# Eight time-step products on whole fp32 tiles that GpSimd adds, in place of sixteen on high and low parts

## What is computed

```python
h = rmsnorm(x, p['norm1_g']) * (1 + sc1) + sh1
u, q, k, v, z, xbc, dt_raw = split_sizes(h @ p['w_in'], IN_SIZES)
...
dt = jax.nn.softplus(dt_raw.reshape(b, n, 2, SSD_HEADS) + p['ssd_dt_bias'])
```

## Time and profile before

| | |
|---|---|
| median of 3 runs | 1295.12 us (1294.97 to 1297.24) |
| span of the profiled execution | 1295.7 us |
| TensorE busy | 1275.4 us |
| VectorE busy | 1078.2 us |
| ScalarE busy | 652.1 us |
| GpSimd busy | 183.8 us |

### The profile page before, as it was taken

One profiled execution on the slowest core, in us unless ns is written; L12 is line 12 of the kernel. 1 busy time (PEld: TensorE's weight loads), 2 busy tenths in 40 slices (PEclk: granted clock), 3 DMA queues, 4 the chain that ended last, 5 costly groups with the idle time before them and its releaser, 6 DMA issues.

```text
span 1295.7 us, 20368 instructions
## 1 busy us (share of the span) xinstructions
PE 1275.4 (98%) x7736; PEld 1228.9 (95%) x7736; DVE 1078.2 (83%) x1984; ACT 652.1 (50%) x1098; POOL 183.8 (14%) x187
## 2 busy tenths in 40 slices
PE   6999999999999999999999999999999999999997
PEld 5999899999999999999999988999999999999997
DVE  5899978878987999999968998877988799999433
ACT  5643555555566454543375336555555754554332
POOL 0067000002210000001103910000042000000110
PEclk9999999999999999999999999999999999999999
DMA  9566436544443444458735662464435254444431
GB/s 360 186 235 205 161 115 217 172 150 142 150 146 114 147 163 144 166 177 278 237 111 180 223 211 84 168 233 142 141 129 195 83 167 141 163 136 164 152 127 56
DMA packets 60481, 216.26 MB, mean 167 GB/s; under 512 B 7104, under 2 KB 9408, under 8 KB 58848
## 3 DMA queue, kind: packets, MB, share of 16 engines
q1 hardware_dynamic: 56224, 199.38, 45.4%
q0 software_dynamic: 4016, 15.39, 3.9%
q10 hardware_dynamic: 144, 0.20, 0.0%
HBM read 211.17 MB, written 3.77 MB: 166 GB/s over the span
## 4 chain that ended last, share of the span: by engine, by line
PE 83%; DVE 8%; ACT 5%; issue 2%; DMA 2%; SPq 0%; DVEq 0%; ACTq 0%; POOLq 0%
PE acc L1044 25%; PE acc L1046 25%; PE acc L1045 25%; DVE cv L2001 2%; DVE wl L1820 1%; PE mixes L1315 1%; DMA crow_late<-in_cvec_rows_dram 1%; PE mixes L1219 1%; DMA x<-in_xp_dram 1%; ACT th L1445 1%; ACT hh L1434 1%; PE mixes L1249 1%; DVE junk_late L1909 1%; PE misc L1032 1%; ACT cv L1445 0%
## 5 line engine op out<-in xcount | busy, mean ns | idle before, releaser
L1044 PE MATMUL acc<-hh,wh 128*128 128x384 f32 x1519 | 516.0, 340 | 0.6 <-DVE wl L1820 0.2
L1046 PE MATMUL acc<-hh,wl 128*128 128x384 f32 x1519 | 507.9, 334 | 0.0
L1045 PE MATMUL acc<-hl,wh 128*128 128x384 f32 x1519 | 507.7, 334 | 0.0
L1820 DVE TENSOR_TENSOR wl<-raw,wh 128x1024 fp32r<-128x1024 f32 (+1 forms) x276 | 342.0, 1240 | 72.9 <-ACT wh L1409 71.7
L1409 ACT ACTIVATE wh<-raw 128x1024 fp32r<-128x1024 f32 (+1 forms) x276 | 287.0, 1041 | 134.2 <-PE acc L1046 131.5
L1044 PEld LDWEIGHTS acc<-hh,wh 128*128 128x128 f32 x1519 | 285.2, 188 | 8.5 <-issue 3.4
L1045 PEld LDWEIGHTS acc<-hl,wh 128*128 128x128 f32 x1519 | 285.3, 188 | 1.5
L1046 PEld LDWEIGHTS acc<-hh,wl 128*128 128x128 f32 x1519 | 285.2, 188 | 0.0
L2001 DVE SCALAR_TENSOR_TENSOR cv<-acc,prm,cv 128x1 f32<-128x1 f32 (+1 forms) x416 | 153.7, 411 | 9.0 <-ACT cv L1572 1.9
L1046 PE MATMUL acc<-ah,wl 128*128 128x384 f32 x352 | 117.6, 334 | 0.0
L1044 PE MATMUL acc<-ah,wh 128*128 128x384 f32 x352 | 117.6, 334 | 0.0
(11 more groups left out here) (320 smaller groups left out, 1670.4 us busy)
## 6 DMA issues: line engine op xcount, KB each, us to landing
raw<-in_wstream_dram SPq DMA_DIRECT2D x248, 512.0 KB, 3.8
rawm<-in_wstream_dram SPq DMA_DIRECT2D x80, 512.0 KB, 4.3
raw<-in_wstream_dram SPq DMA_DIRECT2D x32, 448.0 KB, 3.7
head<-in_whead_dram SPq DMA_DIRECT2D x8, 1024.0 KB, 15.1
rowf<-runs_dram POOLq DMA_DIRECT2D x12, 256.0 KB, 4.2
rowb<-runs_dram POOLq DMA_DIRECT2D x12, 256.0 KB, 4.8
crow_late<-in_cvec_rows_dram POOLq DMA_DIRECT2D x2, 1024.0 KB, 6.3
crow<-in_cvec_rows_dram POOLq DMA_DIRECT2D x2, 1024.0 KB, 5.3
```

What stands on the lines that cost most here:

```text
L1044: mm(out, sh, mhi, start=start, stop=False)
L1045: mm(out, sh, mlo, start=False, stop=False)
L1046: return mm(out, sl, mhi, start=False, stop=stop)
L1820: tt(wl[:, s, 0:n], raw[:, raw_slot(u), 0:n], wh[:, s, 0:n].bitcast(F32), ALU.subtract).then_inc(lo_done, 1)
```

## The change

GpSimd gets a new step `whole_tiles`, at its places `u` = 4 to 7 in each layer (`WHOLE0`), two tiles at each: it adds `hh` and `hl` of a tile to a plain fp32 tile, in `gates[6]` to `gates[12]` and `ot[0]`, which are free then. `time_steps` waits for all eight and does eight products on them. The names of the semaphore and of the tiles are new; nothing else moves.

```diff
--- before.py
+++ after.py
@@ -246,6 +246,7 @@
 SLOT_PW, SLOT_X, SLOT_A, SLOT_S, SLOT_Y = 4, 14, 17, 17, 19
 SLOT_LN = SLOT_X + 1
 SLOT_WDC = 7
+WHOLE0 = 4
 POOLING = (UU0 + 4, UU0 + 6, UU0 + 9, UU0 + 12)
 
 Y_SLOTS = 2
@@ -466,6 +467,7 @@
         mix7 = mixes[:, 2, :]
 
         dtc = gates[:, 13, :]
+        whole = [gates[:, 6 + k, :] for k in range(KT - 1)] + [ot[:, 0, :]]
 
         head_bank = [(mix7, mix5)[p % 2][:, 8 * (p // 2):8 * (p // 2) + 8] for p in range(KT // 2)]
         wt_bank = (acc[3], misc[:, :])
@@ -568,6 +570,7 @@
         lam_exp = sem("lam_exp")
         lam_sum = sem("lam_sum")
         wd_hi = sem("wd_hi")
+        whole_made = sem("whole_made")
         u_in = sem("u_in")
         pooled = sem("pooled")
         pads = sem("pads")
@@ -763,6 +766,19 @@
                     last = nc.gpsimd.memset(ut[:, :, c0:c1], 0.0)
                 last.then_inc(pads, 1)
 
+            def whole_tiles(l, k0):
+
+                if k0 == 0:
+                    if l:
+                        group_done(pool, l - 1, NG - 1)
+                    else:
+
+                        pool.wait_ge(scale_ready, KT // 2)
+                    pool.wait_ge(h_lo, count(l, NSPLIT, SP_N1 + KT - 1))
+                for k in (k0, k0 + 1):
+                    nc.gpsimd.tensor_tensor(whole[k], hh[:, k, :].bitcast(F32), hl[:, k, :].bitcast(F32), ALU.add) \
+                        .then_inc(whole_made, 1)
+
             def pooling(l, j):
 
                 tmp = [gates[:, 20:22, :].rearrange("p a t -> p (a t)")[:, 0:UW],
@@ -831,6 +847,8 @@
                         lo(l, u + AHEAD)
                     if u == 4:
                         clear_pads(l)
+                    if WHOLE0 <= u < WHOLE0 + 4:
+                        whole_tiles(l, 2 * (u - WHOLE0))
                     if u in POOLING:
                         pooling(l, POOLING.index(u))
                     if u == MIX0 + 8:
@@ -1164,11 +1182,10 @@
                 misc_turn(l, M_DT)
 
                 pe.wait_ge(par_ready, l + 1)
-                for half, src in enumerate((hh, hl)):
-                    for k in range(KT):
-                        g = 32 * (k % 4)
-                        last = mm(mz[g:g + 32, :], wd[:, k, :], src[:, k, :].bitcast(F32),
-                                  start=(half == 0 and k < 4), stop=(half == 1 and k >= 4))
+                pe.wait_ge(whole_made, KT * (l + 1))
+                for k in range(KT):
+                    g = 32 * (k % 4)
+                    last = mm(mz[g:g + 32, :], wd[:, k, :], whole[k], start=(k < 4), stop=(k >= 4))
                 last.then_inc(misc_done, 1)
 
             def time_transposes(l):
```

## The result

| | median of 5 runs | span of the profiled execution |
|---|---|---|
| before | 1295.78 us (1294.97 to 1297.24) | 1295.7 us |
| after | 1304.28 us (1303.87 to 1304.47) | 1302.2 us |

The ratio of the runs is 1.0066, with a 95% interval of 1.0056 to 1.0077: slower by 8.5 us, above the forecast range (1293.2 to 1299.4), and above the 1298.9 of rival 1 as well.

The account below looks back on a forecast made before the run. TensorE, busy 1275.4 of 1295.7 us, was taken as the bound. Layer 0 +2.6, layer 1 +1.5 and saving -2.2 gave +1.9 us: 1297.0 us, no change that can be told, range 1293.2 to 1299.4.

Parts of the forecast that it names:

- rival 1: Layer 0: small parameter instructions take turns with adds too, `nlam` 3.3 us late, layer 0 costs 4.5; 1298.9 us, chance 0.28.
- the start of layer 0: Layer 0, XBC stage: adds 1 and 2 make `nlam` 1.2 us late, and with it the first evacuation, taps and `wl`.
- The start of the adds: GpSimd, layer 0: adds begin once the pads are cleared, by 47.73, after a set-up taken as short.
- the price for a small one: Small VectorE parameter instructions, layer 0: may or may not take turns, between nothing and 0.87 us per add then running.
- the 50.5: Sign in layer 0: the prediction is wrong if `nlam` comes past 50.5.
- the walk: Layer 0 up to unit 6: `nlam` 1.2, `wl` of unit 4 0.5, `xbc` behind it 0.9 late; +2.6 us.
- Layer 1: XBC stage of layer 1: unit 3 waits 1.2 us longer; unit 6 is 1.5 us late, including the 1.2.
- The lock rule: GpSimd adds and VectorE instructions with two SBUF inputs exclude each other for a whole instruction; 0.87 us per add met.
- The saving: Time steps: eight products fewer, 1.31 us a layer, 1.1 kept; 2.2 us in all, bounds 2.0 and 2.6.
- Rivals 3 and 4: Adds do not hurt, 1292.5 to 1292.9 us, chance 0.08; time-step saving is not there, 1299.2 us, chance 0.04.
- The set-up: GpSimd instruction between pads and first add, layer 0: between nothing and 26.9 us, taken as short.
- rival 2: Layer 0: set-up of 8 us or more, adds too late to harm, cost 0.4 us; 1294.8 us, chance 0.12.

Follow-up runs that it names:

- own_wait: The changed kernel, with GpSimd also waiting ahead of the adds for the semaphore of its own memsets; 1297.66 us in a single run.
- lam_sum: The changed kernel, with the adds also waiting for VectorE's sum over `lamt`; 1297.87 us timed, ratio 1.0019 to the kernel before.
- after_params: The changed kernel, with GpSimd's adds also waiting until that layer's parameter instructions are through (`nlam`); 1298.70 us, ratio 1.0024.
- eight_only: The changed kernel without adds or the wait for them, eight products on the high parts `hh` only; 1293.18 us, ratio 0.9981.
- small_mid: `after_params` plus one small two-input VectorE sum between the first taps and `wl`, in the midst of the adds; 1299.96 us in a single run.
- sum_behind: The changed kernel, with VectorE's product and sum over `lamt` put behind the four halvings, GpSimd unchanged; 1305.24 us in a single run.
- late6: The changed kernel, with each layer's adds waiting until VectorE has made the weights `wl` of unit 6; 1293.04 us, ratio 0.9982.
- one_gap: The changed kernel, with GpSimd waiting for its own semaphore once per layer, behind the first add; 1301.05 us in a single run.

## Why the prediction was wrong

**The step that failed** is the one on the start of layer 0: "Adds 1 and 2 then hold off the last small parameter instructions: `nlam` [...] comes 1.2 us late". The start of the adds was right: 45.34 is, to 0.02, the forecast 47.73 less the 2.41 by which this execution is ahead. But the step took for granted that a held VectorE instruction gets its turn behind the add in progress, and the price for a small one was bounded by 0.87 for each add then running. It got its turn behind the eighth, 7.6 us late. `nlam` ended at 53.72, past the 50.5 that the prediction named as a sign of its being wrong, TensorE waited 7.05 us at unit 4, and its clock fell to half. The layer 0 stretch cost 9.26 us where 2.6 was forecast: 7.2 at the wait, and 2.0 net behind it at half clock. Rival 1 looked at the right instructions and thought of turns with them (3.3 us late); turns are not what happened.

**With that step as assumed, the term is right.** Where GpSimd stops ahead of its first add (`own_wait`), two small instructions wait for one add each, and the walk comes out term by term: `nlam` ends 1.5 late (forecast 1.2), the first `wl` loses 0.5 (0.5) and the `xbc` behind it 0.8 (0.87). Layer 0 costs 2.84, for the 2.6 forecast; `lam_sum` costs 2.93, and its 1297.87 stands beside the 1297.0. In `after_params` the price is 3.99, of which 1.5 is clock: that is a term which the prediction put at nothing. From the earlier trace rows it took the clock for full; what a wait of 2 us does to it, no row of before showed. That `own_wait` and `lam_sum` come so near the forecast is luck in one respect: their waits of 1.3 to 1.4 us left the clock full.

**Layer 1** was forecast at +1.5 and cost 1.67, of which 1.2 at unit 3, as forecast: `wl` pieces of 1.35 and 1.21, then a `wl` of 1.58 and an `xbc` of 1.37, and a wait of 1.60 at unit 3 in place of 0.40. The lock rule of the Trainium skill (SBUF — State Buffer, Who interferes with whom) agrees with the trace here, and with `after_params`. In layer 0 it is right that the two exclude each other, but blocking the second to issue, for one instruction, is not enough to give the 7.80 us: the halving was recorded 0.02 ahead of the first add, and 0.11 with three more memsets, and had to let eight of them pass.

**The saving** was forecast at 1.31 a layer with 1.1 kept. `eight_only` saves 1.29 and keeps 1.04 of it to 250, and 0.84 in layer 1: 1.9 together by the products (1.67 over all stretches of the table), and 2.5 by the ratio of its runs, with 1.3 to 3.6 as the interval. The 2.2 forecast stands between. Rivals 3 and 4 fell: adds do hurt, the saving is there.

**The set-up** was taken as short, and is: the first add begins at 45.34, with the memsets ending at 45.31. The Trainium skill (GPSIMD Engine Reference, 2.1 Instruction dispatch) speaks of about 6 us at the first call; the trace shows nothing of it at this place, and rival 2, which needed late adds, fell with it.

Put together from the table: 9.26 - 1.29 - 0.02 + 1.67 - 1.29 + 0.51 = +8.84, and the runs say +8.5.

**What stays open** is why a running-on GpSimd shuts out what asks ahead of its first add, while an instruction that asks in the midst of the adds gets the next boundary (all of layer 1, and `small_mid`). The profile has no row for who holds what. Nor do I know why the sum at 45.12 ran its ordinary 0.29 us beside the memsets, while a halving issued ahead of them was held in `sum_behind`. The kernels show that a wait of GpSimd ahead of the adds ends it, not by what.

## What to carry to other kernels

Work on an idle engine isn't free because that engine is idle: ask which instructions of the busy engine it meets, and put it where that engine is ahead of the one that waits for it. Here the same sixteen adds cost 10.9 us (9.26 + 1.67) as first placed, and 0.02 once they waited for the weights of unit 6. If a run of GpSimd instructions must start beside VectorE work that is urgent, try a semaphore wait of GpSimd right ahead of it, even for one of its own: that line alone was worth some 6 us here, by one run and its profile. In two of the six kernels that wait there (`own_wait` and `lam_sum`) halvings stood right ahead of the first add and went through. And a small instruction can be the dearest of a chain, so look at the longest time of a row and not only at the large ones.

## What the runs showed of the hardware

- A run of eight GpSimd adds, going on from memsets without a stop, held a VectorE instruction of 0.17 us for 7.80 to 7.89 us in seven profiles, and three instructions took 8.04 to 8.10 in `sum_behind`; a stop of 0.1 to 0.2 us for a semaphore prevented or ended it.
- Taking turns makes a row of adds longer as well: seven take 6.79 us alone, and beside `wl` and `xbc` 9.03 (layer 1 of the changed kernel), 9.12 (`after_params`) and 9.62 (`late6`).
- A wait of TensorE of 2.13 us (`after_params`) was followed by the half clock up to 65.5, 3.4 us from the first product on, and one of 7.05 us by a half clock that lasted until 62.5, 5.2 us from the first product on. Eleven products in the wait kept it at full. Waits of 7.04 to 7.34 us in six other profiles were followed by 3.0 to 5.6 us of half clock, a wait of 2.28 us in `one_gap` by none, and the waits of 1.36 and 1.33 in `own_wait` by none: the length of a wait alone doesn't give its price.
